# Two transformer blocks in one hand-ordered Trainium2 kernel: other orders on VectorE and ScalarE, other homes for intermediates, expert weights requested at other points

## The reference

```python
# first block
proj = rms_norm(x) @ w_in                       # q, k, v, u, gate logits
merged = gate_attn * (stick_breaking_attention(q, k, v) @ w_branch_attn) \
       + gate_ssm * (s5_branch(u) @ w_branch_ssm)
x = x + rms_norm(merged @ w_out)
x = x + rms_norm(memory_cross_attention(rms_norm(x), rms_norm(mem)))
up = causal_conv(rms_norm(x) @ w_up, width=3) + conv_b      # 2 x 2816 wide
gate, val = split(up)
x = x + rms_norm((gelu(gate) * val) @ w_down)
# second block
q, k, v, o, i, f, u_g, v_g = split(rms_norm(x) @ w_in2)
h_m = sigmoid(o) * mlstm(silu(conv4(q, k)), v, i, f)        # 4 heads
gated = gelu(u_g) * (w_spatial * tri) @ rms_norm(gelu(v_g)) # 8 groups
x = x + concat(head_rms(h_m), head_rms(gated)) @ w_out2
# 32 experts (4 groups of 8), top 2 of the chosen group, no token dropped
x = x + sum_e weight_e * ((silu(xn @ w_gate[e]) * (xn @ w_up[e])) @ w_down[e])
out = rms_norm(x, final gain)
```

## Time and profile before

| | us |
|---|---|
| runs | 1140.66, 1149.1, 1150.58 |
| median | 1149.1 |
| the profiled execution | 1148.06 |
| its span in the profile | 1146.2 |
| busy PE | 1098.3 (96%) |
| busy DVE | 648.3 (57%) |
| busy ACT | 395.7 (35%) |

### The profile page before, as it was taken

One profiled execution on the slowest core, in us unless ns is written; L12 is line 12 of the kernel. 1 busy time (PEld: TensorE's weight loads), 2 busy tenths in 40 slices (PEclk: granted clock), 3 DMA queues, 4 the chain that ended last, 5 costly groups with the idle time before them and its releaser, 6 DMA issues.

```text
span 1146.2 us, 17639 instructions
## 1 busy us (share of the span) xinstructions
PE 1098.3 (96%) x6992; PEld 803.2 (70%) x6992; DVE 648.3 (57%) x1312; ACT 395.7 (35%) x662; POOL 6.0 (1%) x21
## 2 busy tenths in 40 slices
PE   8989999999998999999999999999999999999995
PEld 5978778987898999999789995444444444444442
DVE  5999996746467899988888852222222222222213
ACT  5512336336354555556584321111111111111112
POOL 2000000000000000000000000000000000000000
PEclk9999999999989999999999999999999999999998
DMA  7534223453244566665453479999999999999994
GB/s 294 181 132 145 92 93 128 148 170 125 74 148 166 172 223 224 238 226 189 146 185 111 148 318 419 420 420 422 420 421 419 421 420 421 420 421 421 420 419 181
DMA packets 56547, 302.61 MB, mean 264 GB/s; under 512 B 6544, under 2 KB 7440, under 8 KB 31888
## 3 DMA queue, kind: packets, MB, share of 16 engines
q1 hardware_dynamic: 53712, 290.74, 65.4%
q10 hardware_dynamic: 2752, 10.72, 2.7%
HBM read 300.39 MB, written 1.05 MB: 263 GB/s over the span
## 4 chain that ended last, share of the span: by engine, by line
PE 71%; DVE 12%; DMA 11%; ACT 3%; issue 2%; SPq 0%; ACTq 0%; DVEq 0%
PE psum L1945 70%; DMA arena<-in_experts 5%; DVE w_low L1102 3%; DVE arena L1102 3%; DMA sq<-in_experts 2%; DMA spare<-in_experts 2%; DVE arena L1105 2%; DMA ring<-in_stream 2%; ACT w_high L633 1%; DVE h_low L1102 1%; PE psum L2614 0%; DVE rt L1105 0%; DVE sq L1102 0%; DVE h L1105 0%; ACT arena L870 0%
## 5 line engine op out<-in xcount | busy, mean ns | idle before, releaser
L1945 PE MATMUL psum<-arena 128*64 128x512 f32 (+5 forms) x1448 | 260.1, 452 | 10.9 <-DMA arena<-in_experts 4.0
L1945 PEld LDWEIGHTS psum<-arena 128*64 128x64 f32 (+2 forms) x1448 | 135.6, 162 | 136.3 <-issue 118.0
L1102 DVE TENSOR_TENSOR w_low<-ring,w_high 128x1024 fp32r<-128x1024 f32 x146 | 176.9, 1220 | 28.9 <-ACT w_high L633 28.4
L1945 PE MATMUL psum<-h_high,w_high 128*128 128x256 f32 x528 | 153.0, 290 | 8.8 <-DVE h_low L1102 2.9
L633 ACT CAST w_high<-ring 128x1024 fp32r<-128x1024 f32 x146 | 150.6, 1044 | 26.7 <-DMA ring<-in_stream 21.3
L1945 PE MATMUL psum<-h_high,w_low 128*128 128x256 f32 x528 | 150.2, 284 | 0.0
L1945 PE MATMUL psum<-h_low,w_high 128*128 128x256 f32 x528 | 150.2, 284 | 0.0
L1105 DVE SCALAR_TENSOR_TENSOR arena<-arena,psum 128x512 f32<-128x512 f32 (+1 forms) x44 | 29.1, 662 | 195.9 <-ACT arena L1037 188.8
L1945 PE MATMUL psum<-y_high,w_high 128*128 128x256 f32 x480 | 136.5, 284 | 3.0 <-DVE w_low L1102 2.8
L1945 PE MATMUL psum<-y_low,w_high 128*128 128x256 f32 x480 | 134.9, 281 | 0.0
L1945 PE MATMUL psum<-y_high,w_low 128*128 128x256 f32 x480 | 134.9, 281 | 0.0
(11 more groups left out here) (255 smaller groups left out, 1448.7 us busy)
## 6 DMA issues: line engine op xcount, KB each, us to landing
ring<-in_stream SPq DMA_DIRECT2D x180, 512.0 KB, 3.5
arena<-in_experts SPq DMA_DIRECT2D x88, 1024.0 KB, 26.4
parts<-in_experts SPq DMA_DIRECT2D x27, 1024.0 KB, 26.8
ring<-in_experts SPq DMA_DIRECT2D x27, 1024.0 KB, 26.3
spare<-in_experts SPq DMA_DIRECT2D x16, 1024.0 KB, 26.8
x<-in_experts SPq DMA_DIRECT2D x9, 1024.0 KB, 26.3
sq<-in_experts SPq DMA_DIRECT2D x8, 1024.0 KB, 26.6
h<-in_experts SPq DMA_DIRECT2D x8, 1024.0 KB, 26.4
```

The costliest lines, as they stand in the source:

```text
L1102: return dve.tensor_tensor(o, a, b, op)
L1945: return pe.matmul(o, a, b, start=start, stop=stop, skip_group_check=True)
```

## The change

It changes the order of instructions on DVE, ACT and SP, the memory in which some intermediates lie, and the points at which loads are requested. No product and no elementwise operation is added or taken away, and PE's order is the same.

- **Loads.** `EARLY_LOADS` holds seven places, at j = 5 to 18, the new ones 3 and 4. Load 5 goes with 7 and 8 on ACT, load 17 moves on ACT to after `head_squares(1)`; SP issues only load 6 where it issued 3 to 6. `mixw` is requested by ACT after the FFN loop, behind a new wait `hid_ready >= FT`.
- **Homes.** `ug`, `gm_sq`, `so` lie in `h`, `gm` in the bias and decay buffer `bbd`, `hm`, `qt` in place 6, `mixw`, `hm_sq` below word 6160; `ifr` keeps six rows and reuses rows 0 and 1, the row of ones has a place of its own; the hunks that only follow these homes are left out below.
- **Orders.** Branch merging; the cast and the subtraction of unit `xq` 0 ahead of the norm's last steps; one `weights_low` less ahead of norm 4's squares (that unit is then split by the next `weights_low` call); the first two steps of the FFN; `gT`'s copy and `decay_in` in the second mixer.
- **Output.** Four DMAs of 256 KB, by column half and token half.

```diff
--- before.py
+++ after.py
@@ -107,7 +107,7 @@
 PARAMS = 7
-EARLY_LOADS = {6: 0, 9: 1, 12: 2, 15: 19, 18: 20}
+EARLY_LOADS = {5: 0, 8: 1, 10: 2, 12: 19, 14: 20, 16: 3, 18: 4}
 GATES_AT = {p: PER_PAIR * p for p in range(PAIRS - 1)}
@@ -272,16 +272,16 @@
         hden = view(23936, MH, TT)
-        ug = view(16384, 4, T)
-        so = view(17408, 4, T)
-        hm = view(18432, 4, T)
-        qt = view(18432, 2, 2, T)
-        mixw = view(19456, GG, P)
-        gm = view(19456, 4, T)
-        gm_sq, hm_sq = view(16384, 4, T), view(20480, 4, T)
+        ug, gm_sq, so = h[:, 0:4], h[:, 0:4], h[:, 4:8]
+        hm = view(22528, 4, T)
+        qt = view(22528, 2, 2, T)
+        mixw = view(4112, GG, P)
+        gm = bbd[:].rearrange("p a b (c t) -> p (a b c t)", t=P).rearrange("p (a t) -> p a t", t=T)
+        hm_sq = view(5136, 2, T), view(4112, 2, T)
         headed32, xsq = view(5136, KT, T), view(5136, KT, T)
         bsp = view(20480, 4, P)
-        ifr = view(20992, 10, T, parts=MH)
+        ifr = view(20992, 6, T, parts=MH)
+        row_ones = view(2816, T, parts=MH)
         w_if = bbd[:].rearrange("p a b c -> p (a b c)")[:, 0:KT * 36].rearrange("p (k c) -> p k c", k=KT)
@@ -494,8 +494,7 @@
             sp.wait_ge(op_low, KT)
-            for s in range(3, 7):
-                sp.dma_start(held[s], experts[s]).then_inc(expert_in[s], 16)
+            sp.dma_start(held[6], experts[6]).then_inc(expert_in[6], 16)
             for s in range(9, 16):
@@ -518,10 +517,12 @@
                         sp.dma_start(held[n % HELD], experts[n]).then_inc(expert_in[n % HELD], 16)
-            for tt in range(TT):
-                sp.wait_ge(res_ready[tt], 2)
-                sp.dma_start(out[:, tt], result[:, tt]).then_inc(s_out, 16)
-            sp.wait_ge(s_out, 32)
+            for c in range(2):
+                some = slice(c * 512, c * 512 + 512)
+                for tt in range(TT):
+                    sp.wait_ge(res_ready[tt], c + 1)
+                    sp.dma_start(out[:, tt, some], result[:, tt, some]).then_inc(s_out, 16)
+            sp.wait_ge(s_out, 64)
@@ -652,7 +653,6 @@
-                act.dma_start(mixw, dram["mixw"]).then_inc(s_par2, 16)
                 for g in range(2):
@@ -805,14 +805,17 @@
             weights_high(UNIT_AT["bs", 3] + 1)
+            weights_high(UNIT_AT[("out", 0)] + 1)
             for i in range(4):
...
                 act.mul(two(hh, i), two(merged, i), 0.125).then_inc(merged_high, 1)
-                weights_high(UNIT_AT[("out", i)])
+                if i < 2:
+                    weights_high(UNIT_AT[("out", i + 1)] + 1)
             weights_high(UNIT_AT[("out", 0)] + SPLIT_RING)
...
+            weights_high(UNIT_AT[("xq", 0)] + 1)
             gained_inputs("xa_pre", hh, 0, 3)
@@ -860,7 +863,7 @@
             act.copy(rb[:], STAT[:, T:2 * T]).then_inc(mem_spread, 1)
-            for j in range(FT):
+            def conv_begun(j):
                 b = j % 3
@@ -870,6 +873,13 @@
                 ins.then_inc(acc_in, 1)
+
+            for j in range(FT):
+                b = j % 3
+                if j != 1:
+                    conv_begun(j)
+                if j == 0:
+                    conv_begun(1)
                 weights_high(max(UNIT_AT[("fv", j)] + 1 + SPLIT_RING, HIGHS.get(j, (0, 0))[0]))
@@ -881,6 +891,8 @@
                 act.activation(fs[:, b, 0], fs[:, b, 0], ACT.Tanh, scale=GELU_K * GELU_C).then_inc(gelu_th, 1)
+            act.wait_ge(hid_ready, FT)
+            act.dma_start(mixw, dram["mixw"]).then_inc(s_par2, 16)
             weights_high(UNIT_AT["v2", 2] + 1)
@@ -911,7 +923,6 @@
             act.wait_ge(if_ready, 1)
-            act.dma_start(held[17], dram["experts"][17]).then_inc(expert_in[17], 16)
             link(act.activation(ifr[:, 2], ifr[:, 1], ACT.Abs))
@@ -953,19 +964,19 @@
                 act.wait_ge(hm_ready, 2 * i + 2)
-                act.activation(two(hm_sq, i), two(hm, i), ACT.Square).then_inc(hsq, 1)
+                act.activation(hm_sq[i].rearrange("p a t -> p (a t)"), two(hm, i), ACT.Square).then_inc(hsq, 1)
...
             act.wait_ge(if_rows, 1)
-            act.activation(ifr[:, 7], ifr[:, 7], ACT.Exp).then_inc(em_ready, 1)
+            act.activation(ifr[:, 1], ifr[:, 1], ACT.Exp).then_inc(em_ready, 1)
             weights_high(UNIT_AT["qk2", 1] + 1)
...
             evict_ug(1)
-            weights_high(UNIT_AT["qk2", 5] + 1)
             act.wait_ge(gt_done, 1)
...
                      ).then_inc(x_freed["act"], 1)
+            weights_high(UNIT_AT["qk2", 5] + 1)
             gelu_tanh(FT + 4, two(ugs, 1))
@@ -991,10 +1002,11 @@
             evict_o(1)
-            for s in (7, 8):
+            for s in (7, 8, 5):
                 act.dma_start(held[s], dram["experts"][s]).then_inc(expert_in[s], 16)
...
             head_squares(1)
+            act.dma_start(held[17], dram["experts"][17]).then_inc(expert_in[17], 16)
             operand_high(yh[:, 0:2], headed32[:, 0:2], 2)
@@ -1442,16 +1454,20 @@
                     weights_low("bs", i)
-            for i in range(4):
-                states_gated(i)
-                if i:
-                    merged_rest(i - 1)
-                if i >= 2:
-                    weights_low("out", i - 2)
+            states_gated(0)
+            states_gated(1)
+            merged_rest(0)
+            weights_low("out", 0)
+            states_gated(2)
+            merged_rest(1)
+            merged_rest(2)
+            weights_low("out", 1)
+            states_gated(3)
             merged_rest(3)
...
             norm_scale(2)
+            weights_low("xq", 0)
             add_gained(2, "out", "xa_pre", hh, hl, 0)
@@ -1500,7 +1516,6 @@
             link(dve.memset(up[:, :, :, 0:4], 0.0))
-            weights_low("fg", 1)
             squares_added_between(4)
@@ -1522,9 +1537,10 @@
             scaled_up(0)
+            scaled_up(1)
             for j in range(FT):
                 b = j % 3
-                if j:
+                if j >= 2:
                     scaled_up(j)
...
@@ -1607,8 +1623,6 @@
             weights_low("qk2", 4)
-            dve.wait_ge(*pb.read(("ug", 1)))
-            gelu_inner(two(ug, 1), two(ugs, 1))
@@ -1668,10 +1682,12 @@
-            gelu_twice(FT + 4, two(ug, 1), two(ugs, 1))
             dve.wait_ge(*xb.read(("gT", 0)))
             decay_in(0)
+            dve.wait_ge(*pb.read(("ug", 1)))
+            gelu_inner(two(ug, 1), two(ugs, 1))
             decay_in(1)
+            gelu_twice(FT + 4, two(ug, 1), two(ugs, 1))
             weights_low("qk2", 5)
...
```

16 lines of the change are left out of this document (8 added, 8 removed).

## The result

| | before | after |
|---|---|---|
| median | 1146.38 (six runs, 1140.66 to 1150.58) | 1131.83 (six runs, 1130.18 to 1135.01) |
| the profiled execution, its span | 1148.06, 1146.2 | 1131.74, 1129.9 |

The ratio on record is 0.9883, with a 95% interval of 0.9859 to 0.9906: 13.4 us faster (10.8 to 16.2); the two medians themselves lie 14.6 apart. I had forecast 1136 against a median of 1149.1, a ratio of 0.9886. So the change in time came out as forecast; its parts did only in part.

The account below looks back on a forecast made before the run. It took DMA to set the end, clocked from the first place PE gives back (load 21's landing). Earlier first release 11.5, queue 2.0 and tail 0.3 sum to 13.8 us: 1135.3 from median 1149.1, rounded to 1136; range 1127 to 1145.

Parts of the forecast that it names:

- Rival 4: Expert part: end not tied to first release, DMA stream loses the time again; only queue and tail count, 1147; chance 0.08.
- Part 1: Loads ahead of load 21: three fewer in the queue let it land sooner, 2.0 us (ends 0 and 3.7); FFN price 0.
- Rival 3: FFN loop: seven early loads starve the weight stream, 17.5 lost against 13.8 won, 1153; chance 0.04.
- Part 2: Branch merging: third low part 1.85 earlier plus 1.7 from half clock, −3.5 us (ends −1.85 and −4.1).
- Part 3: First unit of xq: cast and subtraction ahead of the norm's last steps remove PE's wait, −1.0 us (ends −0.5, −1.0).
- Part 4: Norm 4: one subtraction less ahead of the squares closes the gap, plus some clock, −2.0 us (ends −0.5 and −4.5).
- Part 5: FFN start: moving scaled_up(1) ahead removes most of the 2.92 gap, a later one grows; −2.8 us (ends −1.0, −4.5).
- Part 6: FFN end: ACT waits for hid_ready ahead of v2's casts; 0, up to +1 if DVE is late.
- Part 7: Second mixer: earlier gT copy and exponents save 1.1 plus a third of the clock's 3.4; −2.2 us (ends −0.8, −4.5).
- Part 8: Output: four 256 KB DMAs, first column halves sent while the second are computed, −0.3 us (ends +0.4 and −0.7).
- rival 1: Dense part: each gap that becomes small takes its half clock stretch along, 18.6 us in all, 1130.5; chance 0.18.
- rival 2: Dense part: DVE's chain only moves the gaps and half clock stays; 5.8 plus 2.0 from the queue, 1141; chance 0.25.

Follow-up runs that it names:

- e1: Changed kernel with loads 3, 4 and 5 put back to SP behind the dense part's stream; median 1133.69, ratio 0.9891 to the kernel before.
- e2: Changed kernel with the old orders at merging, xq, norm 4, FFN start and mixer; 1142.1, ratio 0.9976 to the kernel before.
- e3: Changed kernel with old orders, old places of loads 3 to 5 and old output; new homes, mixw and load 17 requests stay; 1143.53, ratio 0.9985.
- e5: Changed kernel with branch merging in the old order on DVE and ACT; median 1136.49, ratio 0.9903 to the kernel before.
- e12: Changed kernel with the first xq unit's cast and subtraction behind the norm's last steps and output in two 512 KB DMAs; median 1132.47, ratio 0.9882.
- e6: Changed kernel with the one subtraction ahead of norm 4's sums of squares put back; median 1133.86, ratio 0.9894 to the kernel before.
- e7: Changed kernel with FFN step 1 begun as before (scaled_up(1) and conv_begun(1) in their loop places); median 1134.29, ratio 0.9894.
- e11: Kernel before with one edit, load 17 requested later, after head_squares(1); median 1143.93, ratio 0.9988 to the kernel before.
- e8: Changed kernel with the second mixer's gT copy, decay_in and gated branch in the old order; median 1131.91, ratio 0.9873 to the kernel before.
- e4: Changed kernel with 25 instead of 5 small unused products ahead of PE's wait for the router's selection; 1134.38, ratio 0.9896.
- e9: Changed kernel with 14 instead of 5 small unused products ahead of PE's wait for the router's selection; 1131.72, ratio 0.9889.
- e10: Changed kernel with unit fv 4's cast and subtraction moved into FFN idle times and six small-table requests spread over steps 7 to 17; 1133.06, ratio 0.9894.

## Why the prediction was right, and where it wasn't

**What bounds the kernel.** Held. (The first product of the experts' weights stands at 693.81 in the kernel before and at 679.24 after; about 668, as given ahead of the prediction, is where the router begins, with 667.51 for its first product of 36 columns.) The distance from the issue of load 21 to the landing of load 187 is 422.2 to 423.0 in all ten traces with the new loads, while that issue moves by 10.6 us, and 424.6 to 426.2 in the four with the old loads. What the dense part wins reaches the end whole. Rival 4 falls.

**Part 1, the loads: 2.0.** The profiles of before and after give 424.6 − 422.5 = 2.1; the runs that differ in the loads alone (e1) or in loads and output (e2 against e3) 3.7 and 3.1. The sum's value is at the low end of this. The working was half right: load 21 lands 3.9 sooner after its issue, the upper end, and the stream behind it gives 1.8 back, which I hadn't seen; I had the right size by counting bytes. The prediction's "some 4 us ahead of load 21's landing" was a misreading too: the last load of the queue, issued at 683.69, lands at 701.86, 2.5 ahead of it. The price in the FFN was nothing, as taken: from 382 to 518 us PE is busy 135.98 of 136.00, with a DMA share of 0.70 instead of 0.65. Rival 3 falls.

```profile
382.00:518.00 136.00, 135.98 (x1159) 135.78 (x1158) 125.29 (x215) 77.74 (x115) 0.00 (x0) 1.00 0.70 239
```

**Part 2, merging: 3.5.** Measured 3.5 (e5, e2, e3), gap and clock both.

**Part 3, xq: 1.0.** Measured 1.3 (e12).

**Part 4, norm 4: 2.0.** Measured 3.2 alone (e6), 2.3 to 3.1 with the other orders old as well: a term mis-sized by 0.3 to 1.2. I let the clock give 0.9 of its 3.4 because I couldn't tell what the small products there tolerate; the stretch hung on this one subtraction.

**Part 5, FFN start: 2.8.** Measured 2.9 (e7); with the spread of the executions at this place, 2.0 to 3.3. The later gap of 2.5 was forecast and is 2.56, but it isn't what the order costs (e2 and e3 have it with the old one).

**Part 6, FFN end: 0.** Against e11, which requests mixw at step 3 and has no half clock there either, the changed kernel loses 0.1 between 517 and 582 us.

**Part 7, mixer: 2.2.** Measured 0.0 to 0.2: the step that failed. I read the two gaps and the 6.83 us at half clock of one trace as the work of the order. With the same old order e2, e3, e8 and e11 have one gap of 1.0 to 1.2, no other run has the stretch of 6.83 there, and the one of 3.41 comes with either order. The profiled pair does show 3.6 at this place, so a reader of two traces alone would have called the term under-sized.

**Part 8, output: 0.3 gained.** Measured 0.1 lost, inside my ends. Of the Trainium skill's two rules the fit in "DMA: Bandwidth & Descriptors", section "Anatomy of one DMA — SWDGE (gpsimd) path", would have had 0.6 gained, an estimate from its 3.2 and 2.6 us; this case's traces have 3.1 and 2.8. The two column halves are ready within 0.2 us of each other, so there was next to nothing to win by sending one sooner.

Adding the measured parts: 3.5 + 1.3 + 3.2 + 2.9 + 0.1 + (2.1 to 3.7) − 0.1 = 13.0 to 14.6, against 13.4 (10.8 to 16.2); with the lowest readings of norm 4 (2.3) and the FFN start (2.0) it would be 11.2. So the sum of 13.8 came out right by luck in part, by errors against each other: the mixer 2.1 and the output 0.4 too high, norm 4 and the loads together up to 2.9 too low. ("All ends together (5 to 23)" leaves out the two ends on the slow side, 1 at the FFN's end and 0.4 at the output; with them it is about 3.) The 16.3 between the two profiled spans have other things in them that no part makes (below); rivals 1 and 2 are each wrong as a whole: the half clock goes at the merging and norm 4 and not at the mixer.

## What to carry to other kernels

Where a stream of loads with a fixed number of places sets the end, find the first place that is given back: in these traces everything that came ahead of it counted whole, on any engine. (No run here changed the work between that point and the last landing.) A stretch at half clock in one trace is not yet a cost of the code beside it; ask whether it returns with the edit put back, in several traces, and whether a wait behind it swallows it, as at the FFN start and the router here. And a gap that is removed in a chain that bounds (here DVE's at the start of the FFN) is only won if the next step of the chain isn't late by the same amount.

## What the runs showed that I had not expected

- **The half clock is partly the execution's.** At the merging and at norm 4 it comes with the order in every trace. Near 370, 535 and 590 us it comes in some executions of the same order and not in others: e5, e8 and e12 have stretches at 370 to 375, 534 to 539 and 588 to 593; e2 and e6 have none after 400 but the router's. By place one near 590 costs 1.5 (e5, e12), one of 6.83 near 535 costs 1.2 (e1), the others there 0.1 to 0.5.
- **TensorE has two paces in the FFN.** The products are the same 128x256 at full clock, but between 400 and 500 us the one kind of trace has 1.1% more of them than the other. One group of them before, then after (count, busy, mean ns):

```profile
L1945 PE MATMUL psum<-y_low,w_high 128*128 128x256 f32 x186 | 52.2, 281 | 0.0
```

```profile
L1961 PE MATMUL psum<-y_low,w_high 128*128 128x256 f32 x188 | 52.6, 280 | 0.0
```

From start to start a product takes 118.67 ns in the kernel before and in e1, e5 to e8, e11 and e12, and 117.33 in the changed kernel and in e2 to e4, e9 and e10: two values and nothing between, with old and new orders and loads on either side. Over the 997 products from 400 to 517 us that is 1.3 us, and it stands in the difference of the two profiled spans. What chooses the pace stays open.
- **The changed kernel's own profile is not one of its best.** Against e6, e7 and e10 it is 1.1 us later by 20 us of the span and loses 2.1 between 650 us and load 21. All distances in the tables are counted from it, so the places are to be trusted more than the spans.
